# A ring of six slots in place of ten, and the output projection of a layer kept in SBUF for its four tiles

## The reference, cut to what matters

```python
def token_mixer(h, w_in, w_out, mix_gain, ...):
    proj = h @ w_in
    ...                                  # dilated attention, S5 scan, latent attention
    y = jnp.concatenate([rms_norm(ya, ...), rms_norm(yb, ...), rms_norm(yc, ...)], axis=-1)
    return y @ w_out

def peer_ffn(h, wq, subkeys, u_tab, v_tab):
    q = (hf @ wq).reshape(T, PEER_HEADS, 2, PEER_DKEY // 2)
    scores = jnp.einsum('thjd,hjkd->thjk', q, subkeys).astype(jnp.float32)
    top_s, top_i = lax.top_k(scores, PEER_TOPK)
    cand = top_s[:, :, 0, :, None] + top_s[:, :, 1, None, :]
    best_s, best_c = lax.top_k(cand.reshape(T, PEER_HEADS, PEER_TOPK * PEER_TOPK), PEER_TOPK)
    ...                                  # experts: T x 128 indices, gates: softmax of best_s

    def block(args):
        xt, et, gt = args
        act = jax.nn.gelu(jnp.einsum('td,tkd->tk', xt, u_tab[et]).astype(jnp.float32))
        return jnp.einsum('tk,tkd->td', gt * act, v_tab[et].astype(jnp.float32))

def reference(x, c, ...):
    c_act = jax.nn.silu(c)
    for l in range(DEPTH):
        mod = c_act @ w_ada[l] + b_ada[l]
        sh1, sc1, g1, sh2, sc2, g2 = jnp.split(mod, 6, axis=-1)
        h = rms_norm(x, norm1_gain[l]) * (1.0 + sc1[:, None]) + sh1[:, None]
        y = token_mixer(h, w_in[l], w_out[l], ...)
        x = x + g1[:, None] * y
        h = rms_norm(x, norm2_gain[l]) * (1.0 + sc2[:, None]) + sh2[:, None]
        x = x + g2[:, None] * peer_ffn(h, peer_wq[l], peer_subkeys[l], peer_u[l], peer_v[l])
    return x
```

## Time and profile before

| | |
|---|---|
| median of 3 runs | 3313.14 us (3309.66 to 3314.4) |
| the profiled execution | 3310.64 us |
| its span, first to last instruction | 3308.8 us |
| busy, share of the span | PE 72%, DVE 70%, ACT 44%, POOL 34% |
| moved by DMA | 1328.61 MB, mean 402 GB/s |
| gathers | 1024, 1073.81 MB |
| granted TensorE clock | 0.841 of full |

### The profile page before, as it was taken

How to read it: one execution, slowest core, us unless ns; L and a number is a source line. 1 busy time by engine, 2 the same in 40 slices (tenths; PEclk the granted TensorE clock), 3 DMA queues, 4 the chain that set the end, 5 groups by cost and what they waited for, 6 DMA issues and landing times.

```text
span 3308.8 us, 45391 instructions
## 1 busy us (share of the span) xinstructions
PE 2367.5 (72%) x15412; PEld 1175.1 (36%) x15412; DVE 2300.8 (70%) x6374; ACT 1452.3 (44%) x4685; POOL 1137.5 (34%) x1028
## 2 busy tenths in 40 slices
PE   7667777687776788667776777767677588775555
PEld 5454334243341434333343333424234143441111
DVE  5279646897569875797357975588757886579554
ACT  2324543345434465344443445334543445434443
POOL 0013333334333334333233333333333333334442
PEclk9878888788897989879888788888888697887777
DMA  8579999999999999999999999999999999999997
GB/s 312 200 283 403 418 421 419 421 417 419 420 419 407 416 409 393 419 420 419 420 420 419 403 419 420 419 413 418 416 420 412 406 411 405 420 419 395 419 421 331
DMA packets 203869, 1328.61 MB, mean 402 GB/s; under 512 B 24093, under 2 KB 38349, under 8 KB 49014
## 3 DMA queue, kind: packets, MB, share of 16 engines
q0 software_dynamic: 147456, 1073.81, 78.6%
q1 hardware_dynamic: 56182, 251.91, 19.2%
HBM read 1321.41 MB, written 6.51 MB: 401 GB/s over the span
## 4 chain that ended last, share of the span: by engine, by line
DMA 41%; DVE 24%; PE 18%; ACT 6%; issue 5%; POOL 2%; POOLq 0%; ACTq 0%; SPq 0%; DVEq 0%
DMA ringbuf<-in_p_uv,IDX 38%; DVE ringbuf L1652 11%; PE PS L881 9%; POOL ringbuf L554 2%; DMA WB<-in_p_wi 2%; PE PS L673 2%; ACT v_th L1193 2%; PE PS L848 1%; PE PS L820 1%; DVE I L1545 1%; ACT DIAG L1205 1%; ACT v_w L1198 1%; DMA BM<-skew 1%; DVE T L1543 1%; DVE EQ L1589 1%
## 5 line engine op out<-in xcount | busy, mean ns | idle before, releaser
L554 POOL DMA_INDIRECT ringbuf<-in_p_uv,IDX x1024 | 1137.3, 1111 | 2142.5 <-PE PS L881 1768.7
L881 PE MATMUL PS<-ringbuf,DIAG 64*64 64x512 f32 x8192 | 1288.5, 756 | 744.0 <-ACT DIAG L1205 721.1
L1652 DVE SCALAR_TENSOR_TENSOR ringbuf<-ringbuf,H 128x1024 f32<-128x1024 f32 x1024 | 1234.3, 1222 | 642.9 <-DMA ringbuf<-in_p_uv,IDX 612.7
L881 PEld LDWEIGHTS PS<-ringbuf,DIAG 64*64 64x64 f32 x8192 | 310.4, 157 | 1448.0 <-ACT DIAG L1205 987.2
L1190 ACT ACTIVATE v_sq<-v_y 128x2 f32<-128x2 f32 x512 | 104.1, 203 | 1401.6 <-DVE ringbuf L1652 1381.0
L1198 ACT ACTIVATE v_w<-v_th,v_g 128x1 f32<-128x1 f32 x1024 | 340.8, 380 | 48.0 <-ACT v_th L1193 0.4
L1193 ACT ACTIVATE v_th<-v_sq,v_y 128x1 f32<-128x1 f32 x1024 | 340.3, 379 | 17.2
L1205 ACT ACTIVATE DIAG<-fold,v_w 128x64 f32<-128x64 f32 x1024 | 300.8, 341 | 16.7
L848 PEld LDWEIGHTS PS<-HT,WB 128*128 128x128 f32 x1856 | 223.3, 200 | 64.2 <-issue 51.0
L848 PE MATMUL PS<-HT,WB 128*128 128x128 f32 x1856 | 234.1, 287 | 1.6 <-DMA WB<-in_p_wq 1.5
L673 PE MATMUL PS<-WB,HT 128*128 128x256 f32 (+2 forms) x816 | 181.9, 379 | 48.7 <-DMA WB<-in_p_wi 48.7
(11 more groups left out here) (277 smaller groups left out, 2228.2 us busy)
## 6 DMA issues: line engine op xcount, KB each, us to landing
WB<-in_p_wq SPq DMA_DIRECT2D x58, 1024.0 KB
WB<-in_p_wi SPq DMA_DIRECT2D x37, 1024.0 KB
WB<-in_p_ada SPq DMA_DIRECT2D x36, 1024.0 KB
WB<-in_p_wo SPq DMA_DIRECT2D x30, 1024.0 KB
ringbuf<-in_p_uv,IDX POOLq DMA_INDIRECT x1024
WF<-in_p_ada SPq DMA_DIRECT2D x12, 1024.0 KB, 8.8
WB<-in_p_wi SPq DMA_DIRECT2D x14, 768.0 KB
SKT<-in_p_sk SPq DMA_DIRECT2D x64, 128.0 KB
```

Of the source, the lines that this page charges most:

```text
L554: pool.indirect_dma_start(out=ring[n % RING], out_offset=None, in_=table, in_offset=bass.IndirectOffsetOnAxis(ap=IDX[:, k % 2, s:s + 1], a ...
L881: mm = pe.matmul(PS[half:half + HALF, 2 * c + r, :], DIAG[r * HALF:(r + 1) * HALF, (n + q) % DIAGS, :], row[r * HALF:(r + 1) * HALF, D + c ...
L1652: dve.scalar_tensor_tensor(row, row, GELU_T, H2[:, k % 2, :], ALU.mult, ALU.mult, accum_out=Y[:, b, q:q + 1]).then_inc(dotted, 1)
```

## The change

RING is 6. The 32 KB a partition that four slots held become `KEEP`, four chunks (KEPT = 4). `keep(l)` loads the four `wo` chunks of a layer once: for layer 0 beside the attention of tile 0, for layer 1 in tile 4, right behind the first two `wi` chunks and the load of `XM`. PE reads `wo` from `KEEP` in all four tiles of the layer, with the semaphores `keep_in` and `keep_done`. The `wo` chunks leave `chunk_order()`, so later chunks alternate between the two places of `WB` with other numbers. The small tiles have (RING + 1) // 2 = 3 places. `WF` now lies in slots 2 to 5 of the ring, so two gathers, not six, are issued before the chunks of tile 0 are used. The work of the engines is otherwise the same, instruction for instruction.

```diff
 LOT = BATCH * TOPK
 PAIRS = SLOTS // 2
-RING = 10
+RING = 6
+KEPT = 4
 FIRST = 4
...
         else:
             order += wi + [("uk", j, 0), ("glu", j, 0)] + ada
-        order += [("wo", j, i) for i in range(4)] + [("wq", j, i) for i in range(8)]
+        order += [("wo", j, i) for i in range(KEPT, 4)] + [("wq", j, i) for i in range(8)]
     return order
...
         CS = place("CS", [P, SJ, P])
         WB = place("WB", [P, 2, CHUNK])
+        KEEP = place("KEEP", [P, KEPT, CHUNK])
         SKT = place("SKT", [P, 2, 2 * P])
...
         DEN = place("DEN", [P, 2 * HEADS])
         RDN = place("RDN", [P, 2 * HEADS])
-        Y, SQY, TH, G, W = (place(f"v_{s}", [P, RING // 2, 2]) for s in ("y", "sq", "th", "g", "w"))
+        Y, SQY, TH, G, W = (place(f"v_{s}", [P, (RING + 1) // 2, 2]) for s in ("y", "sq", "th", "g", "w"))
         SU = place("SU", [P, BATCH])
...
         ring_in = [sem(f"ring_in{b}") for b in range(RING)]
         w_done = sem("w_done")
+        keep_in, keep_done = sem("keep_in"), sem("keep_done")
         ad_dot, ad_ev, ad_mm, ad_out, ad_gain, modc = (
...
                     src, w = a[f"p_{kind}"][l, :, i * CHUNK:(i + 1) * CHUNK], CHUNK
                 sp.dma_start(weights(n)[:, 0:w], src).then_inc(w_in[slot[n]], 16)
+
+            def keep(l):
+                if l:
+                    sp.wait_ge(keep_done, KEPT * T * l)
+                for i in range(KEPT):
+                    sp.dma_start(KEEP[:, i, :], a["p_wo"][l, :, i * CHUNK:(i + 1) * CHUNK]).then_inc(keep_in, 16)
 
...
                 l, t = divmod(j, T)
                 mine = order[16:18] if j == 0 else order[number[("wi", j, 0)]:number[("glu", j, 0)] + 1]
-                late = order[number[("glu", j, 0)] + 1:number[("wo", j, 2)]]
+                late = order[number[("glu", j, 0)] + 1:number[("wq", j, 0)]]
                 for c in mine:
...
                     if c == ("wi", j, 1):
                         load_x(j)
+                        if j == T:
+                            keep(1)
                         if j >= 2:
...
                 sp.wait_ge(y_mm, 2 * (j + 1))
                 for b in range(HEADS + 1):
-                    if b == 2:
+                    if b == 2 and len(late) > ahead:
                         chunk(late[ahead])
...
                     sp.dma_start(BM[:, m % 2, 0:n], bass.AP(skew.tensor, b * P * (TOEP + 1) + P - 1 + S - n, [[TOEP, P], [1, n]]))\
                         .then_inc(bm_in[m % 2], 16)
-                    if 2 <= b <= len(late) - ahead:
+                    if 2 <= b < len(late) - ahead + 1:
                         chunk(late[ahead + b - 1])
+                    if j == 0 and b == HEADS:
+                        keep(0)
                 for c in late[ahead + HEADS:]:
                     chunk(c)
                 if j == 0:
-                    for c in [("wo", 0, 2), ("wo", 0, 3), ("wq", 0, 0), ("wq", 0, 1)]:
+                    for c in [("wq", 0, 0), ("wq", 0, 1)]:
                         chunk(c)
...
                     keys(0, 7)
                 else:
-                    chunk(("wo", j, 2))
-                    chunk(("wo", j, 3))
                     for i in range(8):
...
                 for i in range(4):
                     yield at(j, 35 + i)
-                    n = number[("wo", j, i)]
-                    pe.wait_ge(w_in[slot[n]], turn[n])
+                    if i < KEPT:
+                        pe.wait_ge(keep_in, 16 * KEPT * (l + 1))
+                        wt, used = KEEP[:, i, :], keep_done
+                    else:
+                        n = number[("wo", j, i)]
+                        pe.wait_ge(w_in[slot[n]], turn[n])
+                        wt, used = weights(n), w_done
                     if i == 0:
...
                         pe.wait_ge(wo_res, 4 * j + i - 1)
                     for k in range(KD):
-                        last = pe.matmul(PS[:, 6 + i % 2, 0:WIDE], HT[:, k, :], weights(n)[:, k * WIDE:(k + 1) * WIDE],
+                        last = pe.matmul(PS[:, 6 + i % 2, 0:WIDE], HT[:, k, :], wt[:, k * WIDE:(k + 1) * WIDE],
                                          start=(k == 0), stop=(k == KD - 1))
-                    last.then_inc(w_done, 1)
+                    last.then_inc(used, 1)
                 yield at(j, 41)
...
             def pair(k, i):
                 m = PAIRS * k + i
-                b = m % (RING // 2)
+                b = m % ((RING + 1) // 2)
                 act.wait_ge(dotted, 2 * m + 2)
...
                     yield at(j, 36 + i)
                     cols = slice(i * WIDE, (i + 1) * WIDE)
-                    dve.wait_ge(w_done, number[("wo", j, i)] + 1)
+                    if i < KEPT:
+                        dve.wait_ge(keep_done, KEPT * j + i + 1)
+                    else:
+                        dve.wait_ge(w_done, number[("wo", j, i)] + 1)
                     if i == 0:
...
             def pair(k, i):
                 m = PAIRS * k + i
-                b = m % (RING // 2)
+                b = m % ((RING + 1) // 2)
                 assert batched >= lots_before(k) + 1 + max(
```

## The result

The changed kernel takes 3541.39 us (median of 4 runs, 3534.55 to 3553.57), the kernel before 3311.4 us (median of 4, run beside it). The ratio is 1.0692, with a 95% interval of 1.0676 to 1.0708. The profiled execution has a span of 3533.3 us and a mean clock of 0.821.

The account below looks back on a forecast made before the run. It took DMA bytes to bound the kernel: 3310.6 us + 112 (ring) + 10 (last tile) + 8 + 5 (single places) - 30 (bytes) = 3415.6, median 3418 us. Likeliest range 3345 to 3510, wider range 3290 to 3590.

Parts of the forecast that it names:

- the turn bounds everything: Rival: with all background in series in the turn, DMA idles a tenth of the time; above 3510, up to 3706 us; chance 0.12.
- the landing: From a pair's first issue to its second gather's landing, empty queue: 8.35 us (8.0 to 8.7), plus 1.6 for weights.
- What is removed: 24 of the 32 `wo` chunk loads go, 25.2 MB, at most 60 us if DMA is the limit there.
- the bytes win: Rival: with landing at 6.8 us or background hidden, the turn stays under DMA time everywhere; -47 us, 3266 us; chance 0.13.
- From the second dot to the next issue: Rest of a slot's turn: 6.3 us, plus 1.84 for half the background; 5.8 to 7.5 in the last tile.
- The turn with background: Seven tiles with background: a turn of 18.1 us against 18.3 available, or 17.9 without the `wo` bytes.
- My +112 us: Ring cost over 448 pairs of seven tiles, 0.25 us a pair from an estimated spread; bounds 0 and +340 us.
- The last tile: Tile without background: a turn of 13.8 to 16.2 us; cost 10 us over 64 pairs, at most 26.
- The saved bytes again: Where the turn is the limit, fewer bytes give nothing; with both limits equal, half counts, -30 us.
- The two single places: Later gathers at the start, +8 us (0 to 17); tile 2's store behind `KEEP` in tile 4, +5 (0 to 10).
- Tile 3 of the kernel before: Support for a rival: 64 pairs took 414 us, read as long attention steps stalling the ring even with ten slots.
- What would show it: Signs: 1303 MB, middle slices under 410 GB/s, some under 390, longer DVE and POOL waits, last tile 324 to 350 us.

Follow-up runs that it names:

- experiment 2: Kernel before, ten slots, but `wo` loaded in tiles 0 and 4 alone, a constant table multiplied in the other tiles: 3250.46 us, ratio 0.9815.
- experiment 4: Changed kernel with two slots in place of six, the freed room left empty: 8778.62 us (one run).
- experiment 1: Changed kernel with six slots but nothing kept, `wo` loaded for every tile as before: 3585.13 us, ratio 1.0827 to the kernel before.

## Why the prediction was wrong

The mechanism was right as far as it went: the turn of a slot with six slots, about the time that DMA needs for three pairs, bytes partly given back. The size was off by a factor of two: 105 us forecast, 230 us measured. The time lies where I had put "the turn bounds everything", with 0.12, but not for the reason given there, background in series: that part of the turn came out shorter than in my sum. The failed step is the landing, a term that was too small. By the steps:

- *What is removed*: right. 60 us with ten slots (experiment 2).
- *The landing* is the step that failed. I took 8.35 us for the second gather, as if the queue were empty. Empty it is 8.85 (experiment 4), just above my upper bound of 8.7 and far above the 6.8 us of the case "the bytes win". With six slots it was 10.6 us in the last tile, and 12.2 us in the others, where I had 9.95 with the weights. The 1.6 us that I added for the weights is about the difference between the two stretches. What I put at nothing, without a reason, is the wait for the other gathers of the ring itself: 1.7 us.
- *From the second dot to the next issue*: 6.3 + 1.84 = 8.1 us forecast in tiles with background, about 7.4 measured, with the wait for DVE in it. Half of the background was too much.
- *The turn with background* was therefore 19.5 us (3 x 6.51), not 18.1. Against 17.9 available it is 0.5 us a pair too long, and 0.50 is what experiment 1 shows. My +112 us (0.25 a pair) rested on equal means and a guessed spread; experiment 1 has +223.
- *The last tile*: +10 forecast, at most 26; +58 measured. The bound failed for the same reason: from the second dot to the next issue 7.1 us lie inside my 5.8 to 7.5, and the landing of 10.6 us lies 1.9 above my 8.7. The lower clock is the smaller part: a pair's matmuls took 3.1 us on the mean in place of 2.9.
- *The saved bytes again*: -30 forecast, -45 measured.
- *The two single places*: no loss to be seen, in the second by luck. In tile 4 the store went out at 1500.80 behind `KEEP` and landed at 1530.79, after 30 us where it took 11.2 before. ACT's Square, which waits for it, began at 1531.07 straight after ACT's work for a pair, so 0.3 us were to spare. The first tile's loss in experiment 1, 32 us, is like that of the others (25 to 37).
- *Tile 3 of the kernel before* was no sign of a ring that stalls. DMA ran at 420 GB/s through all of its 414 us. The stretch is longer because SP's queue moved 37.1 MB in it, against 24.8 in tile 1; 12 chunks of `ada` are the difference.
- *What would show it*: the bytes (1303 MB), a rate under 410 GB/s in most middle slices with some under 390, and longer waits of DVE and POOL came as named. The last tile left the range of 324 to 350 us. The sign for a loss above my range, a doubled wait of DVE for gathers, did not come: 942.1 us are 1.54 times 612.7. `KEEP` went out at 1498, not at about 1421, since the pairs before it had taken longer.

How much one landing differs from the next shows what the mean of 12.2 us hides. Of the 448 pairs of seven tiles, 183 met no bytes of SP's queue on their way, and their second gather landed after 10.2 us on the mean. 58 met more than 2 MB of it and took 16.2 us on the mean. The extreme is the stretch in which `KEEP` is loaded for layer 1, from 1507 to 1527 us; its queues (packets, MB, share of the DMA engines) are these:

```profile
q0 software_dynamic: 598, 4.37, 52.3%
q1 hardware_dynamic: 596, 4.08, 48.8%
```

The gathers' queue (q0) and SP's queue (q1) had nearly the same share, and the pair issued at 1507.40 landed 20.2 us later. The chunks of `KEEP` landed 5 us apart there, and 2.5 us apart in the first tile, where no gathers ran. So in this stretch SP's loads halved the rate of the gathers, and that pair was about 10 us late, more than the 5 us that the prediction gave as the other value beside its 1.6. On the mean of all pairs the 1.6 was right.

Why do pairs wait behind one another while DMA runs dry at other moments? The last tile gives a large part of the answer. Its pairs were issued 2.5 to 9.5 us apart. Of 63, 25 came less than 5 us after the pair before: that pair had still 6 us to go, and theirs landed after 11.2 us on the mean. 21 came over 7 us after it, and landed after 10.0 us and 7 us behind the one before, though DMA needs 5. So bunched pairs wait and spread ones leave DMA with too little to do. PE's matmuls of a pair take 1.95 us or 3.69 us as the clock is granted, which may be one source of the uneven spacing; no run took it away. It also stays open why even the spread pairs took 10.0 us and not 8.85; the pair before them had 3 us to go when they were issued.

## What to carry to other kernels

For a ring, add up the turn of a slot and divide by the slots: it must stay clearly under the time that the bottleneck needs for one, not just meet it. Here DMA needed 5 to 6 us a pair, and a turn of some 18 to 19.5 us had to be covered: with three pairs (six slots) that cost 8.3%, with four (eight slots) 0.7%. Take the landing time from a queue that is as full as it will be, not from an empty one. SBUF for reuse is worth its bytes only as long as the ring keeps the slots that hide the turn: two of ten could be given away here, four could not.

## What was not expected of the hardware

DMA's busy share read 0.97 at 383 GB/s and 0.94 at 352, against 1.01 at 416: the rate fell by 15% and the share by 7%. So near its top the share hardly tells a queue that runs dry from a full one. Further down it tells more, 0.66 at 247 GB/s with four slots. With an empty queue a 1 MB gather landed 5.6 us after its issue, and a second one, issued 1.24 us after the first, 3.2 us behind it (experiment 4), while in the last tile of the kernel with ten slots a gather took 2.5 us.
